# First attention of a two-layer encoder: values as the stationary operand, probabilities normalised before their transposition

## The chip, the cores and the metric

The kernel runs on one core of one Trainium2 chip. The metric is the device time of one execution in microseconds (us). Five engines of the core work side by side and meet at semaphores: TensorE (PE: matrix products, with its weight loads shown as PEld), VectorE (DVE), ScalarE (ACT), GpSimd (POOL) and SyncE (SP, which here starts the loads of weights).

## The reference

A two-layer encoder over 512 tokens with 1024 features, 16 heads of 64. Layer 0 has neighbourhood attention over a grid of 8 rows and 64 columns of tokens, layer 1 sliding-window attention with 4 key and value heads, and each is followed by a squared-ReLU MLP. The first attention is what the change touches:

```python
def neighbourhood_attention(h, w_qkv, rpb, w_o):
    ...
    def row_block(args):
        ...
        s = jnp.einsum('bchd,brckhd->bhcrk', q_r, k_win).astype(jnp.float32)
        ...
        s = s + bias[None].astype(jnp.float32)
        p = jax.nn.softmax(s.reshape(B, N_HEADS, GRID_W, kr * NA_COLS), axis=-1)
        p = p.reshape(B, N_HEADS, GRID_W, kr, NA_COLS).astype(v.dtype)
        return jnp.einsum('bhcrk,brckhd->bchd', p, v_win)
    ...
    return jnp.einsum('bsd,de->bse', o, w_o)
```

Each token sees a window of 8 by 16 grid tokens around it. Results are float32.

## The kernel before

**Numbers in two parts.** Every operand of a product is kept as a high part (`w_hi`, `pt_hi`, ...), which is a cast to the product's type, and a low part (`w_lo`, `pt_lo`, ...), the rest. A product is then high x high + low x high + high x low. ScalarE makes high parts, VectorE low parts, so each operand passes through both.

**Weights.** All weight matrices come as one stream of 180 chunks (128 x 1024) through two buffers `w_raw`. SyncE loads them, ScalarE casts (`w_hi`), VectorE subtracts (`w_lo`); both functions are called `split_weights`. TensorE uses a chunk in 24 products of 512 columns into one of two accumulators `acc`.

**The first attention** is done in steps. Step m makes the query, key and value rows of head pair m (three weight chunks, 3m to 3m+2, `dense_part(0)` to `dense_part(2)`), and does the attention of pair m-1 between these chunks. Steps 1 to 8 attend; step 8 has no chunks of its own but the first part of the output projection in their place. A pair is done in two units g = 0 and 1. A unit is two query tiles j of 128 queries for both heads hh, so four blocks of 128 queries by 256 keys.

For a unit TensorE makes the scores (`na_scores`, into `s_ps`), VectorE adds the bias and finds the largest (`na_logits`), ScalarE takes the exponentials and their sums `rsum` (`na_exp`, in `na_probs`), TensorE transposes the probabilities in eight blocks (`na_transpose`, into `pt_ps`), ScalarE and VectorE split them (`pt_high`, `pt_low`), and TensorE multiplies them with V (`na_values`). The value rows `vT` are transposed to token order in two batches (`na_v_blocks`, into the bank `misc_ps`), and split (`v_high`, `v_low`). In `na_values` the transposed probabilities are the stationary operand, in 16 products of 128 or 64 columns into the bank `o_ps`. VectorE then adds the two halves and divides by the sums (`na_o_sum`: a reciprocal, a reduction, a multiplication into `o_tok`), TensorE transposes the result back to feature order (`transpose_o`), and both engines split it into the operand of the output projection (`na_o_high`, `na_o_low`).

**Order.** Each engine works off one list of instructions, written out by hand in `na_step` of that engine; there is no scheduler. A wait stops everything behind it on its engine. A number such as `o_summed >= 2p` is counted by the semaphore that `then_inc` raises. After step 8, TensorE makes a small table product for the second attention (`t5_product`, in `misc_ps`), then goes on with the output projection.

## Time and profile before

| | us |
|---|---|
| three runs | 1174.11, 1174.2, 1174.97 (median 1174.2) |
| profiled execution | 1175.7 |
| its span, from first to last instruction | 1174.0 |
| TensorE busy in it | 1150.0 |
| VectorE busy | 623.4 |
| ScalarE busy | 466.4 |
| GpSimd busy | 129.6 |
| one step of the first attention (scores to scores, 110.99 to 136.25) | 25.26 |
| mean granted clock of TensorE | 0.996 of full |

The first attention takes the span from about 32 to 235 us. A product's row in a timeline lasts longer than the interval to the next one, since products are pipelined: what a block costs is read from start to start. Busy shares are means over the whole span and say nothing about a block; the waits and the timeline of a step do.

### The profile page before, as it was taken

How to read it: one execution, taken by the hardware profiler on the slowest of the kernel's cores; microseconds unless marked ns; L12 is line 12 of the kernel's file. 1: busy time of each engine (PE TensorE's matmuls, PEld its weight loads, DVE VectorE, ACT ScalarE, POOL GpSimd, SP SyncE). 2: the span in 40 equal slices, each digit the busy share in tenths (PEclk: the TensorE clock that was granted, in tenths of full speed). 3: DMA queues.
4: the chain of work that ended last, by engine and by line, in shares of the span. 5: the costliest groups of instructions: out<-in, count | busy, mean ns of one | idle time of the engine just before them, and what ended most of it. 6: DMA issues, size and time to landing. Idle time of an engine off the chain costs nothing.

```text
span 1174.0 us, 16835 instructions
## 1 busy us (share of the span) xinstructions
PE 1150.0 (98%) x5770; PEld 949.1 (81%) x5770; DVE 623.4 (53%) x988; ACT 466.4 (40%) x811; POOL 129.6 (11%) x243
## 2 busy tenths in 40 slices
PE   6999999999999999999999999999999999999996
PEld 4788888877888888888888788887888888888886
DVE  7676666575443324444345788766544233454335
ACT  6445545344342213433223666644443122443221
POOL 4734332050000000000000122100000000000000
PEclk9999999999999999999999999999999999999998
DMA  7422221142223223232232122122222323223222
GB/s 199 119 70 83 67 85 54 56 133 94 104 89 106 92 91 106 89 103 85 98 107 90 51 63 63 34 71 90 104 93 90 107 89 104 92 90 106 90 89 90
DMA packets 36850, 106.74 MB, mean 91 GB/s; under 512 B 8224, under 2 KB 10544, under 8 KB 36816
## 3 DMA queue, kind: packets, MB, share of 16 engines
q1 hardware_dynamic: 31680, 98.98, 25.2%
q0 software_dynamic: 4992, 7.29, 2.8%
q8 instruction: 21, 0.34, 0.1%
q14 instruction: 13, 0.11, 0.0%
q10 hardware_dynamic: 144, 0.02, 0.0%
HBM read 102.92 MB, written 3.34 MB: 91 GB/s over the span
## 4 chain that ended last, share of the span: by engine, by line
PE 91%; DVE 3%; issue 1%; POOL 1%; ACT 1%; SPq 1%; DMA 1%; DVEq 0%; ACTq 0%; POOLq 0%
PE acc L364 26%; PE acc L366 25%; PE acc L365 25%; PE s_ps L436 3%; PE o_ps L469 2%; PE o_ps L466 2%; PE pt_ps L626 1%; PE pt_ps L457 1%; DVE w_lo L967 1%; SPq L262 1%; PE misc_ps L469 1%; PE misc_ps L426 1%; POOL bias_pairs L292 1%; PE s_ps L364 1%; PE misc_ps L466 1%
## 5 line engine op out<-in xcount | busy, mean ns | idle before, releaser
L721 ACT CAST w_hi<-w_raw 128x1024 fp32r<-128x1024 f32 x180 | 188.8, 1049 | 416.4 <-PE acc L366 412.5
L364 PE MATMUL acc<-h_hi,w_hi 128*128 128x512 f32 x800 | 324.4, 406 | 10.3 <-DVE sqsum L984 9.8
L366 PE MATMUL acc<-h_hi,w_lo 128*128 128x512 f32 x800 | 313.4, 392 | 0.0
L365 PE MATMUL acc<-h_lo,w_hi 128*128 128x512 f32 x800 | 313.0, 391 | 0.0
L967 DVE TENSOR_TENSOR w_lo<-w_raw,w_hi 128x1024 fp32r<-128x1024 f32 x180 | 221.4, 1230 | 153.1 <-ACT w_hi L721 153.0
L364 PE MATMUL acc<-u_hi,w_hi 128*128 128x512 f32 (+1 forms) x624 | 241.4, 387 | 0.9 <-DVE w_lo L967 0.9
L366 PE MATMUL acc<-u_hi,w_lo 128*128 128x512 f32 (+1 forms) x624 | 239.5, 384 | 0.0
L365 PE MATMUL acc<-u_lo,w_hi 128*128 128x512 f32 (+1 forms) x624 | 239.4, 384 | 0.0
L364 PEld LDWEIGHTS acc<-h_hi,w_hi 128*128 128x128 f32 x800 | 150.9, 189 | 48.6 <-issue 14.2
L366 PEld LDWEIGHTS acc<-h_hi,w_lo 128*128 128x128 f32 x800 | 150.9, 189 | 32.4
L365 PEld LDWEIGHTS acc<-h_lo,w_hi 128*128 128x128 f32 x800 | 151.4, 189 | 29.0 <-issue 1.2
L995 DVE SCALAR_TENSOR_TENSOR scaled<-acc,rstd 128x512 f32<-128x512 f32 x90 | 62.2, 691 | 162.1 <-PE acc L366 161.4
L364 PEld LDWEIGHTS acc<-u_hi,w_hi 128*128 128x128 f32 x624 | 117.2, 188 | 26.0 <-DVE w_lo L967 2.6
L366 PEld LDWEIGHTS acc<-u_hi,w_lo 128*128 128x128 f32 x624 | 117.2, 188 | 23.2
L365 PEld LDWEIGHTS acc<-u_lo,w_hi 128*128 128x128 f32 x624 | 117.3, 188 | 22.5
L765 ACT ACTIVATE probs<-probs,nmax 128x256 f32<-128x256 f32 (+1 forms) x128 | 67.8, 531 | 62.5 <-DVE nmax L1055 62.5
L314 POOL DMA_DIRECT2D bias_pairs<-t_shifted x64 | 32.4, 508 | 466.2 <-ACT esink L895 458.5
L1107 DVE TENSOR_TENSOR x_res<-acc,x_res 128x512 f32 (+1 forms) x39 | 26.9, 691 | 101.1 <-PE acc L366 101.1
L1005 DVE TENSOR_TENSOR u_lo<-scaled,u_hi 128x512 f32 (+1 forms) x80 | 55.3, 691 | 12.6 <-ACT u_hi L757 12.2
L304 POOL TENSOR_TENSOR bias_masked<-bias_pairs,mask 128x256 f32<-128x256 f32 x64 | 45.3, 748 | 91.3 <-DVE nmax L1055 89.3
L757 ACT CAST u_hi<-scaled 128x512 f32 (+1 forms) x80 | 49.7, 621 | 10.2 <-DVE scaled L995 3.0
L1015 DVE TENSOR_TENSOR pt_lo<-pt_ps,pt_hi 128x1024 fp32r<-128x1024 f32 (+2 forms) x48 | 45.8, 954 | 13.1 <-ACT pt_hi L770 13.1
(105 smaller groups left out, 989.1 us busy)
## 6 DMA issues: line engine op xcount, KB each, us to landing
w_raw<-in_wstream SPq DMA_DIRECT2D x180, 512.0 KB, 3.3
bias_pairs<-rpb_shifted POOLq DMA_DIRECT2D x64, 48.0 KB, 3.0
bias_pairs<-t_shifted POOLq DMA_DIRECT2D x64, 48.0 KB, 2.1
x_res<-in_xT SPq DMA_DIRECT2D x8, 256.0 KB, 4.6
out_y<-x_res SPq DMA_DIRECT2D x16, 128.0 KB, 1.8
t_shifted<-vT POOLq DMA_DIRECT2D x16, 31.0 KB, 2.0
rpb_shifted<-rpb_pad SPq DMA_DIRECT2D x8, 45.0 KB, 8.5
rpb_shifted<-rpb_pad POOLq DMA_DIRECT2D x8, 45.0 KB, 5.3
```

Source lines behind the costliest of these rows:

```text
L304: ins = nc.gpsimd.tensor_tensor(bias_m[:, g, i, :, :].rearrange("p c r -> p r c"), rows[:, :, U0[j]:U0[j] + WC], mask[:, j:j + 1, :].to_br ...
L364: nc.tensor.matmul(dst, a[0], b[0], start=start, stop=False)
L365: nc.tensor.matmul(dst, a[0], b[1], start=False, stop=False)
L366: return nc.tensor.matmul(dst, a[1], b[0], start=False, stop=stop)
L436: ins = nc.tensor.matmul(dst(hh), a[s, queries[0], queries[1]], b[s, keys[0], keys[1]], start=start, stop=stop)
L721: nc.scalar.copy(w_hi[:, c.odd, :], w_raw[:, c.odd, :]).then_inc(w_hi_made, 1)
L757: nc.scalar.copy(dst, src).then_inc(tile_hi, 1)
L765: return nc.scalar.activation(src, src, ACT.Exp, bias=nmax[:, slot, i:i + 1], scale=-1.0, accum_out=rsum[:, slot, i:i + 1])
L967: nc.vector.tensor_tensor(w_lo[:, c.odd, :], w_raw[:, c.odd, :], f32(w_hi[:, c.odd, :]), ALU.subtract).then_inc(w_split, 1)
L995: nc.vector.scalar_tensor_tensor(out=dst, in0=order(acc[g.odd][:]), scalar=factor, in1=order(rstd[:]), op0=op, op1=ALU.mult).then_inc(acc_ ...
L1005: nc.vector.tensor_tensor(order[0](dst), order[1](scaled[:, e.odd, :]), order[0](f32(hi)), ALU.subtract).then_inc(tile_split, 1)
L1015: nc.vector.tensor_tensor(pt_lo[:, 0:blocks, :], pt_ps[:, 0:blocks, :], f32(pt_hi[:, 0:blocks, :]), ALU.subtract).then_inc(pt_split, 1)
```

## The change

- `na_values`: the values, high and low part of one head side by side, are the stationary operand (128 columns), and both parts of the transposed probabilities the moving one (2 x 128 columns). A unit takes 8 products of 256 columns. All four combinations of parts come out, in four corners of a block with features down the partitions; the corner low x low isn't used. A unit's outputs now lie in both banks, `o_ps` and `misc_ps`, which become one tile `om_ps`.
- Since outputs already have features on the partitions, `transpose_o` goes for this attention. The corners that lie on the other half of the partitions are copied across by ScalarE (`na_o_shift`, two copies of 64 x 256), and VectorE sums the three corners in four additions on half of the partitions each (`na_o_sum`).
- The division by the sums moves to before the transposition: VectorE's reciprocal (`na_inverse`), then four scaled copies in place by ScalarE (`na_normalise`).
- The exponentials of a unit wait for its first two logits, not all four.
- Because a values block writes both banks, the V transpositions and the table product wait until the outputs before them were read (`outputs_read`, on `o_summed`), and `na_values` of a first unit waits for both V batches.
- The order on the engines is rewritten to fit.

```diff
-        v_hi, v_lo = v_parts[:, :, :, 0, :], v_parts[:, :, :, 1, :]
+        v_quarters = v_parts[:].rearrange("p n h t d -> p n (h t) d")
+        v_hi, v_lo = v_quarters[:, :, 0:4:3, :], v_quarters[:, :, 1:3, :]
...
-        pt_hi, pt_lo = sb("pt_hi", [P, 8, P], F32R), sb("pt_lo", [P, 8, P], F32R)
+        pt_parts = sb("pt_parts", [P, 2, 8, P], F32R)
+        pt_hi, pt_lo = pt_parts[:, 0, :, :], pt_parts[:, 1, :, :]
...
-        o_ps = ctx.enter_context(nc.psum_tensor("o_ps", [P, QT, P], F32))
-        misc_ps = ctx.enter_context(nc.psum_tensor("misc_ps", [P, QT, P], F32))
+        om_ps = ctx.enter_context(nc.psum_tensor("om_ps", [P, 2, QT, P], F32))
+        o_ps, misc_ps = om_ps[:, 0, :, :], om_ps[:, 1, :, :]
...
+            def outputs_read(units):
+                pe.wait_ge(o_summed, units.v)
+
             def na_values(p, g):
                 unit = p * 2 + g
                 pe.wait_ge(pt_split, (unit + 1).v)
-                pe.wait_ge(v_split, (unit + 1).v)
+                pe.wait_ge(v_split, (p * 2 + 2).v)
                 if unit.a >= 1:
-                    pe.wait_ge(o_split, unit.v)
-                for i in range(4):
-                    hh, j = i // 2, 2 * g + i % 2
-                    ins = values(o_ps[:, i, :], [2 * i, 2 * i + 1], [2 * j, 2 * j + 1], hh)
+                    outputs_read(unit)
+                for jj in range(2):
+                    for hh in range(2):
+                        for b in range(2):
+                            ins = nc.tensor.matmul(om_ps[:, jj, 2 * hh:2 * hh + 2, :],
+                                                   v_parts[:, 2 * (2 * g + jj) + b, hh, :, :].rearrange("p a b -> p (a b)"),
+                                                   pt_parts[:, :, 2 * (2 * hh + jj) + b, :], start=b == 0, stop=b == 1)
                 ins.then_inc(pv_done, 1)
...
                     if p.a >= 1:
                         pe.wait_ge(v_split, (p * 2).v)
+                        outputs_read(p * 2)
...
                     na_scores(p, 0)
+                    dense_part(0, 0)
                     na_v_blocks(p, 0)
-                if attend and before:
-                    dense_part(0, 0)
-                    transpose_o(p * 2 + -1, o_ps)
                     dense_part(0, 1)
...
                     na_transpose(p, 1)
-                    dense_part(2, 0)
-                    transpose_o(p * 2, o_ps)
-                    dense_part(2, 1)
+                dense_part(2)
+                if attend:
                     na_values(p, 1)
...
             pe.wait_ge(table_landed, 16 * 2)
+            outputs_read(At(UNITS_NA))
...
+            def na_o_shift(p, g):
+
+                unit = p * 2 + g
+                act.wait_ge(pv_done, (unit + 1).v)
+                if unit.a >= 1:
+                    act.wait_ge(o_summed, unit.v)
+                nc.scalar.copy(o_far[TOP, :, :], om_ps[BOTTOM, :, 0, :])
+                nc.scalar.copy(o_far[BOTTOM, :, :], om_ps[TOP, :, 2, :]).then_inc(o_shifted, 1)
...
             def na_exp(p, g):
                 unit = p * 2 + g
-                act.wait_ge(logits_made, (unit + 1).v)
+                act.wait_ge(na_first_logits, (unit + 1).v)
                 for i in range(4):
+                    if i == 2:
+                        act.wait_ge(logits_made, (unit + 1).v)
                     ins = exponent(na_probs[:, i, :], g, i)
+                ins.then_inc(exp_made, 1)
+
+            def na_normalise(p, g):
+                unit = p * 2 + g
+                act.wait_ge(den_made, (unit + 1).v)
+                for i in range(4):
+                    ins = nc.scalar.activation(na_probs[:, i, :], na_probs[:, i, :], ACT.Copy,
+                                               scale=rden[:, g, i // 2, i % 2, :])
                 ins.then_inc(probs_made, 1)
...
+            def na_inverse(p, g):
+                unit = p * 2 + g
+                dve.wait_ge(exp_made, (unit + 1).v)
+                nc.vector.reciprocal(dens_of(rden, g), rsum[:, g, :]).then_inc(den_made, 1)
+
             def na_o_sum(p, g):
                 unit = p * 2 + g
-
-                def dens(g):
-                    nc.vector.reciprocal(dens_of(rden, g), rsum[:, g, :]).then_inc(den_made, 1)
-                    dve.wait_ge(den_made, (unit + 1).v)
-
-                o_sum(unit, unit, g, o_ps, dens)
+                dve.wait_ge(pv_done, (unit + 1).v)
+                dve.wait_ge(o_shifted, (unit + 1).v)
+                if unit.a >= 1:
+                    dve.wait_ge(o_split, unit.v)
+                nc.vector.tensor_tensor(o_t[TOP, :, :], om_ps[TOP, :, 0, :], o_far[TOP, :, :], ALU.add)
+                nc.vector.tensor_tensor(o_t[BOTTOM, :, :], om_ps[BOTTOM, :, 3, :], o_far[BOTTOM, :, :],
+                                        ALU.add).then_inc(o_added, 1)
+                dve.wait_ge(o_added, (unit + 1).v)
+                nc.vector.tensor_tensor(o_t[TOP, :, :], om_ps[TOP, :, 1, :], o_t[TOP, :, :], ALU.add)
+                nc.vector.tensor_tensor(o_t[BOTTOM, :, :], om_ps[BOTTOM, :, 2, :], o_t[BOTTOM, :, :],
+                                        ALU.add).then_inc(o_summed, 1)
...
             def na_step(m, dense=True, attend=True, before=True):
                 p, c, g = m + -1, m * 3 + CH_NA, m * 3 + GR_NA
                 if attend:
+                    na_logits(p, 0)
                     if before:
                         na_o_sum(p + -1, 1)
-                    na_logits(p, 0)
-                    v_low(p * 2, slice(0, 4))
+                    na_inverse(p, 0)
                     if before:
                         na_o_low(p + -1, 1)
+                    v_low(p * 2, slice(0, 4))
...
                     scale_tile(c, g, e, HD ** -0.5)
-                    split_weights(c + 2)
-                    tile_low(e, u_lo[:, 8 + m.odd, :], u_hi[:, 8 + m.odd, :], (in_tiles, by_tile))
                 if attend:
+                    na_logits(p, 1)
                     pt_low(p * 2, 8)
                     v_low(p * 2 + 1, slice(4, 8))
-                    na_logits(p, 1)
                 if dense:
+                    split_weights(c + 2)
+                if attend:
+                    na_inverse(p, 1)
+                if dense:
+                    tile_low(e, u_lo[:, 8 + m.odd, :], u_hi[:, 8 + m.odd, :], (in_tiles, by_tile))
```

Here is how the order moves at two places. First TensorE at the start of a step from the second on, from the pair's first scores to the second half of the first chunk. L436 (before) and L442 (after) are the scores, L426 and L432 the V transpositions, L478 the output transpositions; a chunk's products are three rows per block. Before:

```order
L436 MATMUL s_ps<-k_hi,u_lo 128x256 x2
L494 ISA
L426 MATMUL misc_ps<-ident,vT 128x128 x4
L377 REGISTER_ALU
L379 REGISTER_ALU
L364 MATMUL acc<-h_hi,w_hi 128x512
```

And the end of that half chunk, before:

```order
L366 MATMUL acc<-h_hi,w_lo 128x512
L478 MATMUL o_ps<-ident,o_tok 128x128 x2
L364 MATMUL acc<-h_hi,w_hi 128x512
```

After:

```order
L442 MATMUL s_ps<-k_hi,u_lo 128x256 x2
L383 ISA
L385 REGISTER_ALU
L370 MATMUL acc<-h_hi,w_hi 128x512
```

And the end of that half chunk, after:

```order
L372 MATMUL acc<-h_hi,w_lo 128x512
L507 REGISTER_ALU
L432 MATMUL om_ps<-ident,vT 128x128 x4
L370 MATMUL acc<-h_hi,w_hi 128x512
```

The V transpositions have moved from right behind the scores to the middle of the first chunk, where the output transpositions were; those are gone.

Second VectorE at the same place, from the weight split that ends the step before. L1055 and L1089 are logits (two rows each), L1023 and L1025 the old sum and division, L1073 to L1078 the new additions. Before (the step's first rows):

```order
L1045 RECIPROCAL rden<-rsum 128x4 [waits pv_done]
L1023 TENSOR_REDUCE o_raw<-o_ps 128x256 [waits den_made]
L1025 TENSOR_TENSOR o_tok<-o_raw,rden 128x2x2x64 [waits o_added]
L1060 REGISTER_ALU
L1055 ISA probs,nmax<-s_ps,bias_masked 128x256 [waits pt_done,scores_done,bias_made]
```

After (from the last of the four logits on):

```order
L1089 ISA probs,nmax<-s_ps,bias_masked 128x256
L1089 ISA nmax 128x1
L1072 REGISTER_ALU [waits o_shifted,pv_done]
L1073 TENSOR_TENSOR o_tok<-om_ps,o_raw 64x256 [waits o_split]
L1074 TENSOR_TENSOR o_tok<-om_ps,o_raw 64x256
L1077 TENSOR_TENSOR o_tok<-om_ps,o_tok 64x256 [waits o_added]
L1078 TENSOR_TENSOR o_tok<-om_ps,o_tok 64x256
L1065 RECIPROCAL rden<-rsum 128x4 [waits exp_made]
L1084 ISA [waits o_hi_made]
```

The previous unit's sum has moved from ahead of the new pair's logits to behind them, and is four instructions where it was two and a reciprocal.

## Rows read from the trace of the kernel before

**Rows 1.** The page's busy times: engine, busy us, share of span, instructions.

```profile
PE 1150.0 (98%) x5770; PEld 949.1 (81%) x5770; DVE 623.4 (53%) x988; ACT 466.4 (40%) x811; POOL 129.6 (11%) x243
```

**Rows 2.** Waits of TensorE, 20 to 220 us: total, times, longest.

```profile
PE pt_ps L457 <- ACT probs L765: 2.0, 1, 2.0
PE o_ps L478 <- DVE o_tok L1025: 0.5, 1, 0.5
PE misc_ps L426 <- DVE vT L995: 0.3, 1, 0.3
```

**Rows 3.** Timeline of TensorE, one step: start, duration, line, what, count.

```profile
94.30 0.39 PE L436 MATMUL s_ps<-k_hi,u_hi 64*128 64x256 f32 x2
...
95.21 0.50 PE L364 MATMUL acc<-h_hi,w_hi 128*128 128x512 f32 x1
95.55 0.40 PE L365 MATMUL acc<-h_lo,w_hi 128*128 128x512 f32 x1
...
100.78 0.22 PE L469 MATMUL o_ps<-v_parts,pt_hi 128*128 128x128 f32 x1
...
102.52 1.06 PE L457 MATMUL pt_ps<-ident,probs 128*128 128x128 f32 x8
103.33 0.48 PE L364 MATMUL acc<-h_hi,w_hi 128*128 128x512 f32 x1
...
105.94 0.39 PE L366 MATMUL acc<-h_hi,w_lo 128*128 128x512 f32 x1
...
106.62 0.40 PE L365 MATMUL acc<-h_lo,w_hi 128*128 128x512 f32 x1
...
109.16 0.22 PE L469 MATMUL o_ps<-v_parts,pt_hi 128*128 128x128 f32 x1
...
110.99 0.39 PE L436 MATMUL s_ps<-k_hi,u_hi 64*128 64x256 f32 x2
```

**Rows 4.** Timeline of VectorE, the same step and the next one's start.

```profile
103.34 1.25 DVE L1005 TENSOR_TENSOR k_lo<-scaled,k_hi 128x512 fp32r<-128x512 f32 x1
...
105.75 1.22 DVE L1015 TENSOR_TENSOR pt_lo<-pt_ps,pt_hi 128x1024 fp32r<-128x1024 f32 x1
...
110.44 1.23 DVE L967 TENSOR_TENSOR w_lo<-w_raw,w_hi 128x1024 fp32r<-128x1024 f32 x1
111.58 0.17 DVE L1045 RECIPROCAL rden<-rsum 128x4 f32<-128x4 f32 x1
...
112.87 0.42 DVE L1055 CUSTOM_DVE_ANT_0 probs<-s_ps,bias_masked 128x256 f32<-128x256 f32 x1
...
114.25 0.69 DVE L1010 TENSOR_TENSOR v_parts<-misc_ps,v_parts 128x512 fp32r<-128x512 f32 x1
```

**Rows 5.** Groups by line, 0 to 240 us: busy us, mean ns of one.

```profile
L1023 DVE TENSOR_REDUCE o_raw<-o_ps 128x256 f32<-128x512 f32 x16 | 11.1, 692 | 0.6
...
L1036 DVE TENSOR_TENSOR u_lo<-o_ps,u_hi 128x256 f32 (+1 forms) x16 | 6.8, 424 | 16.0 <-ACT u_hi L780 15.9
L780 ACT CAST u_hi<-o_ps 128x256 f32 (+1 forms) x16 | 5.8, 364 | 22.5 <-PE o_ps L478 22.5
```

**Rows 6.** Timeline of ScalarE, an exponential and the reading of its accumulator.

```profile
89.17 0.51 ACT L765 ACTIVATE probs<-probs,nmax 128x256 f32<-128x256 f32 x1 [1.25 <-DVE nmax L1055]
89.59 0.18 ACT L765 ACTIVATION_READ_ACCUMULATOR probs<-probs,nmax 128x1 f32 x1
```

**Rows 7.** Timeline of VectorE and TensorE in the first attending step.

```profile
38.01 0.42 DVE L1055 CUSTOM_DVE_ANT_0 probs<-s_ps,bias_masked 128x256 f32<-128x256 f32 x1 [2.89 <-POOL bias_masked L304]
...
50.90 2.33 DVE L967 TENSOR_TENSOR w_lo<-w_raw,w_hi 128x1024 fp32r<-128x1024 f32 x1 [0.32 <-ACT w_hi L721]
...
41.64 1.09 PE L457 MATMUL pt_ps<-ident,probs 128*128 128x128 f32 x8 [2.03 <-ACT probs L765]
```

**Rows 8.** Timeline of TensorE, the table product behind the last values block.

```profile
234.56 0.60 PE L686 MATMUL misc_ps<-onehot_sb,table 32*16 32x257 f32 x2
```

**Rows 9.** Busy times around the first step's stop; after POOL: PEclk, DMA share, GB/s.

```profile
39.60:45.00 5.40, 3.37 (x29) 2.91 (x29) 3.52 (x5) 4.83 (x12) 3.80 (x8) 1.00 0.24 46
```

More of the change, by code:

```diff
@@ L214, in encoder @@
         last_square = probs[:, SEQ:2 * SEQ]
+        o_far = o_raw[:].rearrange("p h j d -> p (h j d)").rearrange("p (j n) -> p j n", j=2)
+        o_t = o_tok[:].rearrange("p h j d -> p (h j d)").rearrange("p (j n) -> p j n", j=2)
+        TOP, BOTTOM = slice(0, HD), slice(HD, P)
         na_probs = probs[:, 0:QT * ROWS * WC].rearrange("p (j n) -> p j n", j=QT)
@@ L465, in low @@
                     def low():
-                        nc.tensor.matmul(dst[:, 0:HD], pt_lo[:, t, :], v_hi[:, n, hh, :], start=False, stop=False)
+                        nc.tensor.matmul(dst[:, HD * hh:HD * (hh + 1)], pt_lo[:, t, :], v_hi[:, n, hh, :], start=False,
+                                         stop=False)
                     if b:
@@ L532, in na_step @@
                     na_transpose(p, 1)
-                    dense_part(2, 0)
-                    transpose_o(p * 2, o_ps)
-                    dense_part(2, 1)
+                dense_part(2)
+                if attend:
                     na_values(p, 1)
-                else:
-                    dense_part(2)
             def output_projection(ch, gr, heads_before, start, bank):
                 early_part(ch, gr, heads_before, start, LAST_OUT)
-                transpose_o(At(heads_before + HEADS - 1), bank)
+                if bank is not None:
+                    transpose_o(At(heads_before + HEADS - 1), bank)
                 early_part(ch, gr, heads_before, LAST_OUT, len(EARLY_BLOCKS))
@@ L794, in na_step @@
                 if attend:
-                    v_high(p * 2, v_hi[:, 0:4, :, :])
+                    if before:
+                        na_o_shift(p + -1, 1)
                     na_exp(p, 0)
@@ L798, in na_step @@
                         na_o_high(p + -1, 1)
+                    na_normalise(p, 0)
+                    v_high(p * 2, v_hi[:, 0:4, :, :])
+                if dense and m.a == 0:
+                    load_sqrt()
+                    deviation(0)
+                if attend:
+                    pt_high(p * 2, 8)
+                    v_high(p * 2 + 1, v_hi[:, 4:8, :, :])
                 if dense:
-                    if m.a == 0:
-                        load_sqrt()
-                        deviation(0)
                     split_weights(c + 2)
@@ L901, in sw_o_high @@
             def sw_o_high(p, g):
-                o_high(p * 2 + (HEADS + g), p, g, False, sw_bank(g))
+                act.wait_ge(ot_done, (p * 2 + (g + 1)).v)
+                nc.scalar.copy(half_blocks(u_hi[:, p.v, :], g), flat(sw_bank(g)[:, 0:2, :])).then_inc(o_hi_made, 1)
             def sw_step(m, before=True, dense=True):
@@ L935, in _ @@
             na_step(At(8), dense=False)
+            na_o_shift(At(7), 1)
             na_o_high(At(7), 1)
@@ L1026, in o_sum @@
                                         rden[:, g, :, :, :].to_broadcast([P, 2, 2, HD]), ALU.mult).then_inc(o_summed, 1)
-            def o_low(done, tile, g, grid, bank):
-                dve.wait_ge(o_hi_made, (done + 1).v)
-                hi, lo, src = f32(u_hi[:, tile.v, :]), u_lo[:, tile.v, :], bank[:, 0:2, :]
-                if grid:
-                    hi, lo = half_tiles(hi, g), half_tiles(lo, g)
-                    src = src.rearrange("p j (r c) -> p j r c", c=QC)
-                else:
-                    hi, lo, src = half_blocks(hi, g), half_blocks(lo, g), flat(src)
-                nc.vector.tensor_tensor(lo, src, hi, ALU.subtract).then_inc(o_split, 1)
```

34 lines of the change are left out of this document (19 added, 15 removed).

## The prediction

> **What bounds the kernel now.** I read the page's busy times first: TensorE is busy 1150.0 of 1174.0 us [rows 1]. That alone doesn't say that it is never late, so I read its waits in the first 200 us after the start, where the first attention lies: three, 2.0, 0.5 and 0.3 us, all of them in the first head pair [rows 2]. From the second pair on TensorE goes from block to block without a gap: one step (one head pair and three weight chunks) takes the 25.26 us of the table above. So a TensorE microsecond that goes is worth a microsecond, until another engine's work comes late. Both have to be counted, since the change shortens TensorE's part and lengthens what VectorE and ScalarE do between its blocks.
>
> **What the change takes from TensorE.** The values block has 16 products, each with a stationary operand of its own, and takes 1.74 us from its first product to the transpositions behind it [rows 3]: 0.109 each. It becomes 8 products of 256 columns. No row shows such a product on 128 rows. From below it costs the 0.109 at which products with fresh stationary operands follow each other now, from above the 0.2275 of a 512-column product (5.57 us for 24, the first interval 0.11 longer, 0.34 [rows 3]). I take half of the latter, 0.114, as the columns are half: 0.91 for the block, **0.83 less**, twice a step. The two transpositions of an output stand between two products whose starts are 0.68 us apart [rows 3] where two plain intervals give 0.46: **0.22 less**, twice a step.
>
> **What waits in its place, at the start of a step.** The four V transpositions move behind half a chunk, and they now need the previous unit's outputs read, because the new values block writes their bank too. Count from the first product of a pair's second values block (109.16 [rows 3]). TensorE would be there after 0.91 (values), 0.09 (the passage to the scores: 110.99 - 109.16 less 1.74), 0.91 (scores [rows 3]) and 2.84 (12 products at 0.228 and a 0.11 longer first interval): 4.75. VectorE: it scales the V rows, splits a weight chunk, and is free at 2.42 (111.58 [rows 4]). The logits of the new pair now come first, four in 1.38 us (112.87 to 114.25 [rows 4]): 3.80, as their scores are done before that. Behind them stand the four half-width additions, which the trace doesn't have. The nearest is the 256-element subtraction that reads PSUM, 0.424 [rows 5], in which 128 partitions or 64 should not matter. From below each costs the 0.345 at which the logits follow each other [rows 4], from above the 0.69 of a reduction over 512 [rows 5]. I take 0.424 for all four, as if none overlapped: 1.70 and 0.04 for the wait in their middle, 5.54, and TensorE starts at 5.59. ScalarE's two shifting copies are no part of this: they start when the values are done (1.1), cost some 0.36 each as today's 256-element copy of an output does [rows 5] and are over at 1.85.
>
> That is a new stop of 0.84 us. From the start of the second values block to the middle of the next chunk, the V transpositions left out on both sides, the old order needs 1.83 + 0.91 + 2.74 and 0.22 for the output transpositions = 5.70, the new one 5.59. So the first half of a step gives **only 0.11**, its stop eats the rest. It occurs seven times (steps 2 to 8).
>
> On the overlap of VectorE's additions the Trainium skill has a rule (VectorE: DVE Perf Modes, section "Two Vector instructions with no wait between them"): an instruction whose operand or output begins in another 32-partition quadrant than the last one's in that memory starts only when all earlier ones have finished. The additions alternate between partitions 0 and 64, so by the rule 0.424 stands; by the 0.345 interval of the rows the chain would be up to 0.3 shorter. No run here shows the rule yet.
>
> **The other two chains.** Second unit of a step, counted from the trace's step at 94.30: TensorE reaches its transpositions 0.91 + 5.57 + 0.91 = 7.39 after the scores begin. Scores are done at 1.1, logits at 2.5 (VectorE takes them before the splits now), the exponentials begin when ScalarE has done the casts ahead of them, near 2.6, and end near 4.6. The reciprocal is queued behind the logits, the P subtraction (1.13), the V one (0.60) and a weight split (1.14 [rows 4]): 5.4, done 5.6. The four normalisations are a scaled copy, which the trace doesn't have either; an exponential is followed by the reading of its accumulator after 0.42 [rows 6]. I take 0.40 each and 0.09 for the last one's end, from above the whole 0.51 of an exponential [rows 6]: done at 7.3. **Slack 0.1**. Then the K side: ScalarE's weight cast follows the normalisations (1.05), VectorE splits (1.14), subtracts K (at most 1.25 [rows 4]), adds (1.74), subtracts P (1.22 [rows 4]): about 6.4 after 7.3, and TensorE wants that P after 0.81 of transpositions (102.52 to 103.33) and 5.61 of products (5.83 to 109.16 less 0.22 [rows 3]), at 7.39 + 6.42 = 13.8. **Slack 0.1 to 0.3.** So the second half of a step gives its full 0.83 + 0.22 = **1.05**, eight times, but with almost nothing in hand. The first unit's normalised values are ready 1.3 before they are wanted, since the stop comes before them. GpSimd's masked bias still starts on the logits' end, and SyncE's weight loads on the splits, of which only the third chunk's comes later, by 4 us, two chunks ahead of its use.
>
> **First step, last step, end.** In the first step the logits come late, at 38.01, and TensorE already waits for the exponentials, till 41.64 [rows 7]. Now they may begin after two logits (38.8) and end at 40.9; reciprocal and normalisations bring 42.8: +1.2. The V split follows on both engines: +0.4. A weight split took 2.33 there [rows 7], which the 0.2 of slack doesn't hold: +0.4. The waits of 0.34 and 0.49 [rows 2] go. Without the weight chunks of a full step the last one has less in hand: +0.3. At the end the table product, which went straight behind the last values block, without a wait [rows 8], waits for the outputs: values done 1.1, shifts 1.85, additions 3.6, against an arrival at 1.0: +2.6, less the 0.83 and 0.22 of this last block: +1.55. During such a stop the clock could fall; the 2.0 us stop of the first step left it at 1.00 [rows 9].
>
> **Sum:** 7 x -0.11 = -0.8; 8 x -1.05 = -8.4; first step -0.83 + 2.0 = +1.2; last step +0.3; end +1.55: **-6.2 us**. The later stages keep their work. Against the profiled execution (1175.7 in all, span 1174.0) that is 1169.5; the median of the runs shown, 1174.2, is 1.5 lower, so 1168.0.
>
> **The rivals.**
> - *Additions overlap* (0.345 each): the first chain is 0.32 shorter, seven times and once at the end, -2.5: 1165.5. For it: every run of VectorE instructions in the rows overlaps. Against: a wait in their middle and changing partitions.
> - *The stops don't show at all*, because the chains are shorter than I count: -0.84 x 7, -2.6, -1.6 and -0.3 more: about 1157.5. Against: the first chain is nearly all rows, 3.80 of its 5.59.
> - *Normalisation binds*: 0.49 each instead of 0.40 makes the second unit 0.26 late past its slack and the K side with it, 8 x 0.3 = +2.4, and a tenth of a microsecond in extra sequencer work per chain does another 1.5: 1170.5 to 1172.5. Against: 0.42 in the row. For: the slack of 0.1.
> - *The other side, slower: half-width additions cost more than full-width ones.* Four stand in the first chain and four on the K side, and each extra x costs 4x at once in the first, 4x - 0.2 in the second: 7 x 4x + 8 x (4x - 0.2) + 4x. It is 6.2 at x = 0.12, so from 0.55 per addition on the change loses; at the 0.69 bound it costs 16: near 1182. For it: nothing in the rows but that the form is new.
> - *A 256-column product costs what a 512-column one does*, its moving operand being two runs of 128: 0.118 x 8 = 0.94 per block, eight times exposed and a little in the other ones: +9, 1177. It decides from 0.19 on. Against: scores products of 256 columns go in pairs, 12 in 0.91 us [rows 3].
>
> **How the numbers follow.** Forecast (stops as counted, additions between 0.36 and 0.45): 0.60, own range 1165.5 to 1170.5. Additions overlapping fully 0.11; no stops 0.06; normalisation binding 0.14, of it a third above 1171.9; slower additions 0.05; dear products 0.04. This measurement can tell about 0.2%, 2.35 us, from no change. Faster, below 1171.9, is then 0.60 + 0.11 + 0.06 + 0.09 = 0.86, of which I take 0.04 off for late work that I haven't seen: 0.82. The two slower cases begin within 0.2%: slower 0.08, the rest, 0.10, within it. The range goes from 1162.0, halfway into the case without stops, to 1172.5, the end of the normalisation case.
>
> **What the changed profile would show.** Values blocks 0.9 us from first product to what follows; no TensorE row that reads o_tok; TensorE waiting 0.7 to 1.0 us for VectorE's o_tok before the first V transpositions, seven times, and 2.6 once before the table product; a period of 24.1 us; waits for probs or P near 0 after the first step, 1.2 in it. Additions at 0.42, starting 0.42 apart; normalisations starting 0.40 apart. The forecast is wrong if the additions or normalisations show other intervals, if a 256-column product is not near 0.114, or if a weight split comes late (I see none: the one now behind the logits ends some 3 us before its chunk).

## The result, and the profile after

The changed kernel takes 1177.84 us (median of 20 runs, 1174.47 to 1179.34), the kernel before 1175.26 (20 runs, 1174.1 to 1176.55): ratio 1.0022, interval 1.0016 to 1.0028. It is slower by 0.22%, where 1168.0 was forecast. (The forecast stood on the three runs of before that are shown above, median 1174.2; the 20 runs have 1175.26, so 1.06 of the miss is the base.) One of the twelve runs of the experiment `e_inverse` took 2926.36 us; its ratio to before leaves that run out, its median of 1173.72 doesn't (the other eleven have 1173.36). TensorE has less to do, as the page's busy row says beside [rows 1], and yet the span grew from 1174.0 to 1176.5:

```profile
PE 1140.4 (97%) x5610; PEld 935.5 (80%) x5610; DVE 639.7 (54%) x1020; ACT 505.2 (43%) x907; POOL 134.7 (11%) x243
```

So 9.6 us of TensorE's busy time went and 12 us of waiting came. Its waits in the changed kernel between 20 and 240 us (total, times, longest), beside [rows 2]:

```profile
PE pt_ps L463 <- ACT probs L811: 5.9, 8, 3.8
PE om_ps L432 <- DVE o_tok L1078: 5.3, 7, 0.8
PE om_ps L697 <- DVE o_tok L1078: 2.8, 1, 2.8
```

The second and third line are the stops that the prediction counted. Of the first line 3.8 stand in the first step, forecast as 3.2 (its 2.03 and 1.2 more); the other seven waits, 0.2 to 0.6 each, were forecast as none. One step on TensorE's timeline, beside [rows 3]:

```profile
97.17 0.39 PE L442 MATMUL s_ps<-k_hi,u_hi 64*128 64x256 f32 x2
...
103.65 1.11 PE L500 MATMUL om_ps<-pt_parts,v_parts 128*128 128x256 f32 x8
105.04 1.09 PE L463 MATMUL pt_ps<-ident,probs 128*128 128x128 f32 x8 [0.28 <-ACT probs L811]
...
111.44 1.11 PE L500 MATMUL om_ps<-pt_parts,v_parts 128*128 128x256 f32 x8
112.48 0.39 PE L442 MATMUL s_ps<-k_hi,u_hi 64*128 64x256 f32 x2
...
116.02 0.39 PE L372 MATMUL acc<-h_hi,w_lo 128*128 128x512 f32 x1
117.13 0.63 PE L432 MATMUL om_ps<-ident,vT 128*128 128x128 f32 x4 [0.72 <-DVE o_tok L1078]
```

From the second values block to the scores it is 1.04 (111.44 to 112.48), where it was 1.83, and to the V transpositions 5.69 (forecast 5.59). But the second unit's transpositions start 1.39 after the values block (103.65 to 105.04) instead of 0.91: 0.48 late, though the row shows only 0.28 of it as idle, since the end of a product's row lies behind the start of the next one. Why it is late, VectorE's and GpSimd's timelines show, beside [rows 4]; the last row gives the four biases' shortest, median and longest time in ns, and when the first and the last of them begin:

```profile
101.50 1.66 DVE L998 TENSOR_TENSOR w_lo<-w_raw,w_hi 128x1024 fp32r<-128x1024 f32 x1
103.08 0.17 DVE L1065 RECIPROCAL rden<-rsum 128x4 f32<-128x4 f32 x1
103.17 1.14 DVE L1036 TENSOR_TENSOR u_lo<-scaled,u_hi 128x512 fp32r<-128x512 f32 x1
...
109.09 0.42 DVE L1077 TENSOR_TENSOR o_tok<-om_ps,o_tok 64x256 f32<-64x256 f32 x1
109.52 0.43 DVE L1078 TENSOR_TENSOR o_tok<-om_ps,o_tok 64x256 f32<-64x256 f32 x1
```
```profile
99.93 3.84 POOL L310 TENSOR_TENSOR bias_masked<-bias_pairs,mask 128x256 f32<-128x256 f32 x4 [6.28 <-DVE nmax L1089]
```
```profile
L310 POOL TENSOR_TENSOR bias_masked<-bias_pairs,mask x4: 751/754/1743, 99.9 to 102.0; 128x256 f32<-128x256 f32 x4
```

GpSimd's masked biases (bias plus mask, four additions of 0.75 each) run from 99.93. VectorE's weight split, 1.23 elsewhere, begins at 101.50, during the third of them, and takes 1.66; the third ends near 102.07, and the split 1.09 later. So it stands still until the third bias has ended. The fourth, begun at 102.0, stands still until the split has ended (1743 ns), and the U subtraction behind the split takes 1.14, not 0.68, in the same way. The reciprocal, which the change makes the way to the second unit's probabilities, is queued behind the split. In the kernel before, the biases ran from 99.19 to 102.03, and the next split began at 102.20. The Trainium skill (SBUF — State Buffer, section "Who interferes with whom") says that a VectorE instruction with two SBUF inputs contends with a GpSimd one that reads SBUF, and that one blocks while the other has the port. By that rule, this trace agrees: each of the two waits out the other here.

The clock fell twice. Windows (busy time with counts of TensorE, its weight loads, VectorE, ScalarE, GpSimd; then TensorE's granted clock, DMA share, GB/s), beside the 1.00 of [rows 9]:

```profile
39.00:45.00 6.00, 2.25 (x11) 1.75 (x10) 2.31 (x11) 4.25 (x13) 4.49 (x9) 0.78 0.11 25
45.00:50.00 5.00, 5.00 (x25) 4.11 (x24) 2.11 (x10) 3.90 (x8) 4.66 (x9) 0.58 0.23 54
50.00:55.00 5.00, 5.00 (x27) 4.25 (x25) 5.00 (x6) 2.13 (x9) 4.12 (x8) 1.00 0.06 10
230.00:235.00 5.00, 2.89 (x16) 2.14 (x14) 4.25 (x7) 2.10 (x4) 0.00 (x0) 1.00 0.40 137
235.00:240.00 5.00, 4.35 (x13) 3.17 (x14) 2.30 (x6) 0.40 (x1) 2.95 (x7) 0.70 0.27 89
```

The first fall is in and behind a stop of 3.75 us, the second behind the one ahead of the table product. TensorE's timeline there, beside [rows 8]: products are 0.43 apart from 236.97 to 240.38, the 1.2 GHz level, where they were 0.23 apart:

```profile
235.65 0.59 PE L697 MATMUL om_ps<-onehot_sb,table 32*16 32x257 f32 x2 [2.77 <-DVE o_tok L1078]
...
237.39 0.63 PE L371 MATMUL s_ps<-u_lo,w_hi 128*128 128x512 f32 x1
237.82 0.63 PE L372 MATMUL s_ps<-u_hi,w_lo 128*128 128x512 f32 x1
```

The first attending step, beside [rows 7], on GpSimd, VectorE and TensorE:

```profile
47.22 5.62 POOL L310 TENSOR_TENSOR bias_masked<-bias_pairs,mask 128x256 f32<-128x256 f32 x8
```
```profile
51.37 2.54 DVE L998 TENSOR_TENSOR w_lo<-w_raw,w_hi 128x1024 fp32r<-128x1024 f32 x1
53.83 0.16 DVE L1065 RECIPROCAL rden<-rsum 128x4 f32<-128x4 f32 x1
```
```profile
43.62 1.97 PE L463 MATMUL pt_ps<-ident,probs 128*128 128x128 f32 x8 [3.75 <-ACT probs L811]
55.79 1.10 PE L463 MATMUL pt_ps<-ident,probs 128*128 128x128 f32 x8 [0.55 <-ACT probs L811]
```

**Where the time went.** The span can be cut at four starts that every trace has: VectorE's first logits, the second step's first scores, the eighth step's first scores (six periods later), and ScalarE's `rstd` of the next norm. What lies behind the last is 902.0 to 902.1 in every kernel.

| | before | after | difference | forecast |
|---|---|---|---|---|
| start to first logits | 38.01 | 38.73 | +0.72 | 0 |
| first logits to second step | 22.48 | 24.52 | +2.04 | -0.7 |
| six periods | 6 x 25.26 | 6 x 24.63 | -3.79 | -7.0 |
| eighth step to `rstd` | 59.96 | 63.47 | +3.51 | +1.5 |

The forecast column is the prediction's sum by these bounds: first step +1.2 - 1.05 - 0.83; periods 6 x -1.16; the rest +0.72 - 1.05 + 0.3 + 1.55. The first row can't be told from the chance of one execution: the first logits wait for GpSimd's biases and those for a DMA, and in the traces of kernels with the same instructions up to there they begin between 36.5 and 38.9.

### The profile page after: what moved, and what is told of

It reads as the page before. It is cut to its first block, busy times and chain, and to the rows that moved or that the text cites. A ratio compares the mean times of both kernels' runs of the same rounds, so it can differ in the third digit from the quotient of the medians.

```text
span 1176.5 us, 16678 instructions
## 1 busy us (share of the span) xinstructions
PE 1140.4 (97%) x5610; PEld 935.5 (80%) x5610; DVE 639.7 (54%) x1020; ACT 505.2 (43%) x907; POOL 134.7 (11%) x243
## 4 chain that ended last, share of the span: by engine, by line
PE 85%; DVE 7%; issue 3%; ACT 2%; POOL 1%; SPq 1%; DMA 1%; DVEq 0%; ACTq 0%; POOLq 0%
PE acc L370 24%; PE acc L371 24%; PE acc L372 24%; PE s_ps L442 3%; DVE probs L1089 2%; PE om_ps L476 2%; PE pt_ps L636 1%; PE pt_ps L463 1%; PE om_ps L472 1%; DVE w_lo L998 1%; ACT probs L811 1%; SPq L268 1%; DVE pt_parts L1046 1%; PE om_ps L432 1%; PE s_ps L370 1%
## 5 line engine op out<-in xcount | busy, mean ns | idle before, releaser
L370 PE MATMUL acc<-h_hi,w_hi 128*128 128x512 f32 x800 | 324.1, 405 | 10.9 <-DVE sqsum L1015 10.4
L998 DVE TENSOR_TENSOR w_lo<-w_raw,w_hi 128x1024 fp32r<-128x1024 f32 x180 | 224.2, 1245 | 155.7 <-ACT w_hi L732 155.6
L1036 DVE TENSOR_TENSOR u_lo<-scaled,u_hi 128x512 f32 (+1 forms) x80 | 58.0, 725 | 12.6 <-ACT u_hi L768 12.2
L310 POOL TENSOR_TENSOR bias_masked<-bias_pairs,mask 128x256 f32<-128x256 f32 x64 | 51.2, 839 | 85.2 <-DVE nmax L1089 82.0
L742 ACT ACTIVATE h_hi<-x_res,gain 128x512 fp32r<-128x512 f32 (+1 forms) x32 | 23.1, 722 | 71.3 <-DVE x_res L1147 62.9
```

The costliest lines, as they stand in the source:

```text
L310: ins = nc.gpsimd.tensor_tensor(bias_m[:, g, i, :, :].rearrange("p c r -> p r c"), rows[:, :, U0[j]:U0[j] + WC], mask[:, j:j + 1, :].to_br ...
L370: nc.tensor.matmul(dst, a[0], b[0], start=start, stop=False)
L998: nc.vector.tensor_tensor(w_lo[:, c.odd, :], w_raw[:, c.odd, :], f32(w_hi[:, c.odd, :]), ALU.subtract).then_inc(w_split, 1)
L1036: nc.vector.tensor_tensor(order[0](dst), order[1](scaled[:, e.odd, :]), order[0](f32(hi)), ALU.subtract).then_inc(tile_split, 1)
```

## The experiments

Unless it says otherwise each is the changed kernel with the edit shown. Medians stand against 1177.84, and the medians of the kernel before that were measured beside them lie between 1175.09 and 1175.43; "first step" and "end" are the second and fourth row of the table above (24.52 and 63.47 for the changed kernel).

| run | median, us | ratio to before (95%) | first step | period | end |
|---|---|---|---|---|---|
| e_fill | 1176.45 | 1.0016 (1.0007 to 1.0024) | 24.54 | 24.63 | 61.74 |
| e_table | 1173.77 | 0.9987 (0.9979 to 0.9996) | 24.55 | 24.62 | 59.13 |
| e_step1 | 1179.62 | 1.0037 (1.0024 to 1.005) | 26.36 | 24.63 | 64.88 |
| e_inverse | 1173.72 | 0.9984 (0.9974 to 0.9993) | 23.50 | 24.14 | 63.43 |
| e_bias | 1175.27 | 0.9998 (0.9989 to 1.0007) | 23.66 | 24.51 | 64.73 |
| e_si | 1172.91 | 0.9981 (0.9972 to 0.999) | 23.00 | 24.14 | 63.42 |
| e_vlate | 1166.94 | 0.9935 (0.9921 to 0.9948) | 24.55 | 23.22 | 62.04 |
| e_best | 1160.56 | 0.9875 (0.986 to 0.989) | 23.50 | 23.12 | 57.73 |
| e_fill_end | 1175.73 | 1.0005 (0.9996 to 1.0014) | 24.52 | 24.63 | 61.75 |
| e_fill_inv | 1172.59 | 0.9974 (0.9964 to 0.9985) | 23.02 | 24.14 | 64.71 |
| e_best2 | 1159.87 | 0.9874 (0.9858 to 0.9889) | 21.01 | 23.13 | 57.72 |
| b_step1 (of before) | 1175.87 | 1.0 (0.9991 to 1.0009) | 22.45 | 25.25 | 59.97 |

**e_fill: work in both long stops.**

```
+            def fill(count):
+                for _ in range(count):
+                    nc.tensor.matmul(flat(pt_ps[:, 0:4, :]), h_hi[:, 0, 0:P], h_hi[:, 0, :], start=True, stop=True)
...
+                    if not before:
+                        fill(15)
                     na_transpose(p, 0)
...
             pe.wait_ge(table_landed, 16 * 2)
+            fill(11)
             outputs_read(At(UNITS_NA))
```

> The changed kernel, with products added whose result nothing reads: 15 of 512 columns while TensorE waits 3.75 us for the first step's probabilities, 11 while it waits 2.77 us ahead of the table product. No wait is removed. Theory 1 (the clock): these two stops left the granted clock at 0.78 and 0.58 in the first step and at 0.70 after the table product; kept busy, TensorE stays near 1.00, the 8 transpositions of the first step take about 1.0 instead of 1.97, and 2.4 + 1.6 = 4.0 us come back: about 1173.8. Rival (the stops cost their own length only, and the work after them is slow for another reason): no change, 1177 to 1178, with the same slow products at about 0.43 behind both.

Measured: -1.4, a third of it. Windows of the trace:

```profile
45.00:50.00 5.00, 5.00 (x24) 4.12 (x23) 5.00 (x11) 2.72 (x10) 4.98 (x8) 1.00 0.10 23
...
235.00:240.00 5.00, 5.00 (x24) 4.12 (x23) 1.93 (x3) 1.05 (x1) 4.97 (x11) 1.00 0.24 52
```

The clock stayed at 1.00 in both places (0.58 and 0.70 without the filling). The end is 1.7 shorter, but the first step is as long as it was (24.54). What TensorE gained there it lost at the second transposition, since the split, started earlier, now stands still for longer (VectorE, then TensorE):

```profile
46.02 1.22 DVE L1053 TENSOR_TENSOR pt_parts<-pt_ps,pt_parts 128x1024 fp32r<-128x1024 f32 x1
...
47.76 4.22 DVE L1005 TENSOR_TENSOR w_lo<-w_raw,w_hi 128x1024 fp32r<-128x1024 f32 x1
```
```profile
53.86 1.09 PE L463 MATMUL pt_ps<-ident,probs 128*128 128x128 f32 x8 [2.83 <-ACT probs L818]
```

Theory 1 falls for the first step and stands for the end. In the twelve traces with GpSimd's eight biases in a row (two of them of the old order), that split ends 1.06 to 1.09 after the last of them, whenever it began: 52.84 and 53.91 in the changed kernel, 50.89 and 51.98 here. As it takes 1.21 to 1.23 alone, it gets next to nothing done while they run. Not every VectorE instruction is held up so: the P subtraction at 46.02, beside the same eight biases (45.28 to 50.89), took its usual 1.22. One of its inputs lies in PSUM, where both inputs of the split lie in SBUF.

**e_fill_end: the end's stop alone filled** (the `fill(11)` of above).

> The changed kernel with 11 products of 512 columns, whose result nothing reads, in the 2.8 us stop ahead of the table product, and nothing else: the stop stays as long, but TensorE has work in it. Theory 1 (the clock): the products behind it run 0.23 apart and not 0.43, and -1.6 us comes back: about 1176.2. Rival (the fall is not what costs): 1177.8. The table product later gave -4.1; with the stop at 2.8, the clock's share would then be the rest, 1.3.

Measured: -2.1, and 1.7 in the profile's end. The clock's price behind this stop is 1.7 of 3.51.

**e_table: the table product behind five blocks of the output projection.**

```
             def output_projection(ch, gr, heads_before, start, bank):
                 early_part(ch, gr, heads_before, start, LAST_OUT)
+                if bank is None:
+                    pe.wait_ge(table_landed, 16 * 2)
+                    outputs_read(At(UNITS_NA))
+                    nc.tensor.matmul(flat(misc_ps[:])[0:HEADS, 0:RELS], table[:], onehot_sb[:], start=True,
+                                     stop=True).then_inc(t5_product, 1)
```

> The changed kernel with one edit: the table product moved behind five blocks of the output projection, so that TensorE has work while the last outputs are added up. Theory 1: the 2.77 us stop goes and the clock's fall of 1.6 us with it: -4.2 us, about 1173.6. If the stop costs its length only: -2.7 us, 1175.1. Rival (the end is bound by something else, such as the table's rows that are written and read back): no change.

Measured: -4.1, in the profile -4.34 at the end, as the theory has it: 1.7 of clock and 2.6 of stop. The end is then 0.8 shorter than before the change.

**e_step1: half of a dense part ahead of the first step's first transposition.**

```
+                if attend and not before:
+                    dense_part(1, 0)
                 if attend:
                     na_transpose(p, 0)
...
-                dense_part(1)
+                if attend and not before:
+                    dense_part(1, 1)
+                else:
+                    dense_part(1)
```

> The changed kernel with one edit, in the first attention step alone: four of the eight pieces of the second dense part come ahead of the first transposition, not behind it. Theory 1: the 3.75 us stop shrinks by their 2.5 to 3 us to about 1 and the clock stays near 1.00: -2.4 for the clock, and up to -2.7 of the stop where nothing later waits in its place: -4 to -5 us, about 1173. Rival (the stop is set by a chain that ends the step anyway, and the clock doesn't matter): -1 or less, with a new wait later in the step.

Measured: +1.8, a miss. The first transposition waits 0.84 only, but the second one, with its cover moved ahead, waits behind a split of 4.19, and now the clock falls behind that stop, where nothing hides it:

```profile
54.18 1.97 PE L463 MATMUL pt_ps<-ident,probs 128*128 128x128 f32 x8 [4.66 <-ACT probs L816]
```
```profile
50.00:55.00 5.00, 0.82 (x4) 0.82 (x5) 3.56 (x4) 2.58 (x6) 3.82 (x8) 0.62 0.36 104
```

Its rival was right: a chain through the other engines ends this step. The second transposition starts 17.09 after the first logits here, 17.11 in e_fill and 17.06 in the changed kernel, whatever TensorE did before it. The 1.8 more come behind it: products at half the clock, with the stop ahead of them 4.66 long, where e_fill had 2.83 and full clock.

**e_inverse: the second unit's reciprocal ahead of the split.**

```
-                if dense:
-                    split_weights(c + 2)
                 if attend:
                     na_inverse(p, 1)
                 if dense:
+                    split_weights(c + 2)
                     tile_low(e, u_lo[:, 8 + m.odd, :], u_hi[:, 8 + m.odd, :], (in_tiles, by_tile))
```

> The changed kernel with one edit: on VectorE the second unit's reciprocal comes ahead of the weight split that took 1.66 us and held it. Theory 2 (the second unit's probabilities are late because this short reciprocal stands behind the stretched split): the start of the second transposition moves forward by about 0.45 us in each of 7 or 8 steps, the short waits ahead of it go, -3.0 to -3.6 us, about 1174.5. Rival A (the exponentials on ScalarE end too late anyway): no change. Rival B (the weight split, now later, holds up the next split or the products that read it): slower, with a new wait on w_lo.

Measured: -4.1. The period falls by 0.483, the lateness read above, and between 60 and 230 us TensorE's waits are one line; that for `probs` is gone:

```profile
PE om_ps L432 <- DVE o_tok L1078: 5.2, 7, 0.8
```

The first step, too, is 1.0 shorter. Rival A falls: the exponentials were in time. The split itself did not move: it ends 3.23 after the first bias begins, in this kernel (97.25 to 100.48) as in the changed one (99.93 to 103.16); only what was queued behind it is free.

**e_bias: GpSimd's second masked bias one unit of logits later.**

```
-                    pool.wait_ge(logits_made, (pair * 2 + (g - 1)).v)
+                    pool.wait_ge(logits_made, (pair * 2 + (1 if g else -1)).v)
```

> The changed kernel with one edit: GpSimd's masked bias of the second unit waits for one unit of logits more, so that it no longer runs beside VectorE's weight split. Theory 2 in full (the split took 1.66 instead of 1.23 us, and 4.2 in the first step of two other kernels, because GpSimd works on SBUF at the same time and one stands still while the other runs): the split is back at 1.23, the reciprocal behind it comes 0.43 earlier, the waits of 0.25 ahead of the second transposition go, and some 0.4 us in each of 7 steps come back: -3 us, about 1175. Rival (the stretch has another cause, such as the reads of TensorE or a DMA): the split still takes 1.66 and the time stays at 1177.8. If the masked biases now meet another VectorE operation that binds: slower.

Measured: -2.6, but the period gave only 0.12 of the 0.4. The biases were held up by the loads ahead of them in GpSimd's queue, and met the same split from the other side: they end at 100.38, and the split again 1.07 later (GpSimd, VectorE). In the first step, where GpSimd does nothing at that time, the split took 1.21:

```profile
97.54 2.84 POOL L310 TENSOR_TENSOR bias_masked<-bias_pairs,mask 128x256 f32<-128x256 f32 x4
```
```profile
50.60 1.21 DVE L998 TENSOR_TENSOR w_lo<-w_raw,w_hi 128x1024 fp32r<-128x1024 f32 x1
...
99.81 1.64 DVE L998 TENSOR_TENSOR w_lo<-w_raw,w_hi 128x1024 fp32r<-128x1024 f32 x1
```

The cause of the stretch is shown by this pair and by the unmoved 1.07; as a remedy for the later steps the edit failed.

**e_si: the edits of e_step1 and e_inverse together.**

> The changed kernel with two edits of earlier runs together: half of the first step's second dense part ahead of the first transposition, and the second unit's reciprocal ahead of the weight split. The first edit alone made it slower (1179.6), with a new stop of 4.66 us at the second transposition, whose reciprocal stood behind a split of 4.19 us that ran beside GpSimd's masked biases. If that is the cause, the reciprocal ahead of the split removes that stop, both long stops of the first step go, the clock stays at 1.00, and it is 4 to 5 us below the reciprocal edit alone (1173.7): about 1169. Rival (the first step is set by what GpSimd makes, whatever the order): within 1 us of 1173.7.

Measured: 0.8 below e_inverse alone, as the rival had it, not the forecast's 4 to 5. The 4.66 us stop is gone (0.56 is left), so it was the reciprocal behind the split. But the products that need the split then wait for it, 1.18 at `w_lo`, and the first step is 23.00, against 23.50.

**e_fill_inv: e_inverse with 16 filling products in the first step's stop.**

> The kernel with the reciprocal ahead of the split (1173.7), with 16 such products in the 4.2 us stop ahead of the first step's first transposition. The reciprocal no longer waits for the stretched split, so the stop at the second transposition that took back what the filling of both stops gave should be small. Theory 1: the clock stays at 1.00 in the first step, where it was 0.57 and 0.75, and -2.4 us comes back: about 1171.3. Rival (the first step ends with GpSimd's masked biases and the split behind them, whatever TensorE's clock): 1173 to 1174, with a wait for w_lo of about 1 us in place of it, as the kernel with both edits of the first step had it.

Measured: 1.1 below e_inverse; first step 23.02 against 23.50, with the clock at 1.00 there and 0.57 and 0.75 without. Once the reciprocal is free, the clock costs 0.5 in the first step, not 2.4.

**e_vlate: V transpositions behind the whole dense part.**

```
                     dense_part(0, 0)
-                    na_v_blocks(p, 0)
                     dense_part(0, 1)
+                    na_v_blocks(p, 0)
...
                     na_transpose(p, 0)
-                    na_v_blocks(p, 1)
                     na_scores(p, 1)
+                    na_v_blocks(p, 1)
```

> The changed kernel with one edit: in each step the first V transpositions come behind the whole first dense part, not in its middle, and the second ones behind the second unit's scores. The seven stops of 0.7 to 0.8 us at the step's start, in which TensorE waits for the output additions of 0.43 us apart, should go. If their cost is their length (as the prediction had it): -0.75 x 7 = -5.3 us, about 1172.5. Rival (a later wait takes their place, for the normalised probabilities or for the split V): half of it or less, with that wait in the list.

Measured: -10.9, twice the forecast. The period fell by 1.40: more than the 0.72 to 0.8 of the stop and the 0.11 longer first interval behind it. The rest, about 0.5, is the size of what e_inverse gave: the second unit's scores now come ahead of four V transpositions, and between them and the transposition that waited there is 0.5 us more of work. That this is the reason is argued and not shown by an edit of its own; the wait for `probs` is gone from the list, though the split still took 1.65 to 1.67 in the six later steps. Between 60 and 230 us one wait is left, ahead of the table product:

```profile
PE om_ps L697 <- DVE o_tok L1078: 2.8, 1, 2.8
```

**e_best: e_table, e_step1, e_inverse and e_vlate together.**

> The changed kernel with all four edits: table product later, half a dense part earlier in the first step, reciprocal ahead of the split, V transpositions later. If the four costs are separate they add up: -4.1 (table, measured) -4.1 (reciprocal, measured) -4.5 (first step, once the reciprocal is free) -5.3 (step starts) = -18: about 1160, and no wait over 1 us between 40 and 240 us. If they share one limit: 1165 or more.

Measured: 1160.56, the forecast's 1160. The trace has no wait of TensorE between 60 and 230 us; the period is 23.12, 0.11 less than with e_vlate alone, so most of what e_inverse gives a period (0.48) is in e_vlate's gain already. The sum of four came out right by luck: the first step gave 1.0 in the profile where 4.5 had been put down for it, and the later V transpositions gave about twice their 5.3. The first step still has stops of 1.45 and 1.90.

**e_best2: e_best and e_bias.**

> The kernel with all four edits (1160.6), and GpSimd's masked bias of the second unit one unit of logits later as well. In the first step this leaves GpSimd idle when the split runs, which took 1.21 us so instead of 3.5 to 4.2: the wait for w_lo (0.64) goes, and the four kernels' second unit is no longer held: -0.6 to -1.5 us, about 1159.5. Rival (the logits now wait for the bias, which comes later): slower, with VectorE idle until GpSimd's bias_masked.

Measured: 1159.87 (1159.02 to 1162.67), with e_best at 1160.56 (1160.19 to 1161.33): no difference that these runs tell. In the profile the first step is 21.01 instead of 23.50, the wait for `w_lo` is gone and its split took 1.20. But the profiled execution is the fastest of the four, with a mean clock of 0.998 where the others have 0.995 to 0.996, and part of the 2.5 is the clock, which fell in the profile of e_best alone.

**b_step1: the kernel before with the edit of e_step1.**

> The kernel BEFORE the change with the first step's edit alone: half of the second dense part ahead of the first transposition, where it had a stop of 2.03 us. It is the fair yardstick for what order alone gives without the change. If the stop costs its length: -2.0, about 1173.1. If the first step ends with GpSimd's masked biases and the split behind them: -0.5 or less. In either case the kernel of before keeps its period of 25.26 us a step, so that the 15 us of the four edits are not to be had without the change.

Measured: no change, first step 22.45 against 22.48. Its stop of 2.03 went, and one of 1.8 came later in the step, for the first unit's outputs:

```profile
PE o_ps L478 <- DVE o_tok L1030: 1.8, 1, 1.8
```

So that step's stop cost nothing before the change either.

## Why the prediction was wrong

**Right:** the products and the additions. The values block costs what was forecast; the additions start 0.42 to 0.47 apart and nothing of them overlaps, which rules out the two rivals on them, as the 1.04 does that of the dear product. By the rule of the Trainium skill that the prediction cites (VectorE: DVE Perf Modes, section "Two Vector instructions with no wait between them"), the trace agrees. Four normalisations take 1.71 us, as forecast, so the rival in which normalisation binds by its own length falls. The chain to the stop at a step's start is as forecast, 5.69 for 5.59 (a stop of 0.72 to 0.8 for 0.84), and e_vlate showed its cost in full. The eighth step up to its last values block takes 20.70 before (212.03 to 232.73) and 20.67 after (211.00 to 231.67), 0.03 less, where +0.72 - 1.05 + 0.3 gives the same; that step has no weight split in the way of its second reciprocal. One slip in the sums changes nothing: additions at the 0.69 bound cost 64 x 0.266 - 1.6 = 15.4, so that rival ends near 1183, not 1182.

**Wrong, step by step:**
1. "a weight split (1.14 [rows 4]): 5.4, done 5.6 ... **Slack 0.1**". The 1.14 was read where GpSimd is idle. The logits of the second unit now come ahead of the split, and it is they that release GpSimd's biases; so they run beside it. The split took 1.66, the reciprocal was late by 0.4, and 0.48 a period was lost: 6 x 0.48 = 2.9 of the 3.2 missed there. Putting the reciprocal first gave back 0.483. The prediction wrote that the bias "still starts on the logits' end" and didn't ask what VectorE would do then.
2. "A weight split took 2.33 there [rows 7] ... +0.4" in the first step. The 2.33 had the same cause; it ended 1.1 after GpSimd's biases. Before the change no probabilities were queued behind it. The step's end was set by the biases, split, reciprocal and normalisations in this order: 2.04 more instead of 0.7 less. The sum had put the late split at +0.4 in all. Neither the 3.75 stop nor the clock's fall behind it costs anything in the changed kernel (e_fill 24.54), and without the reciprocal in that queue the step is 1.0 to 1.5 shorter (e_inverse, e_fill_inv), with the biases away too, 3.5 in one profile (e_best2, with the other edits and in a fast execution; the medians of e_best and e_best2 don't tell the two apart).
3. "During such a stop the clock could fall; the 2.0 us stop of the first step left it at 1.00": the conclusion drawn for a stop of 2.6. It was 2.77 and the clock fell; 1.7 (e_fill_end) of the 2.0 missed at the end.

So step 1 and 2 have one cause, a queue behind an instruction that another engine holds up. They cost some 5.6 of the 8.0 by which the three lower rows of the table miss the forecast; the clock costs 1.7. My own first reading of the result, in which the clock cost 2.4 in the first step too, is refuted by e_fill. What stays open: why in the first step GpSimd's eight biases ran through ahead of the split, while in the later steps the split came in between the third and the fourth; and why, in some of the profiles, the fall at the end costs over 1 us more (end 64.7 to 64.9 in e_step1, e_bias and e_fill_inv).

The change itself was worth making: TensorE's work of a step fell from 25.26 to 23.12, which only shows when nothing waits. The kernel before has no gap in its periods to win by order [rows 2], and its first step didn't gain by it (b_step1). The four edits around the change make it 1.25% faster than before (ratio 0.9875, interval 0.986 to 0.989).

## What to carry to other kernels

When a short instruction becomes the way to the critical engine, look at what stands ahead of it in its queue, and put it ahead of any long one; its slack can't be summed from durations that were read where the engine beside it was idle. When an order moves, ask what its end releases, and which instruction will then run at the same time: in these traces VectorE's subtractions with two SBUF inputs and GpSimd's additions held each other up. A stop's length is its cost only if the next wait isn't already due: fill it and look whether the step gets shorter, before moving work for its sake.

## What the runs showed of the hardware

A VectorE split of 1.23 us (both inputs in SBUF) took up to 4.22 beside GpSimd's additions, and ended 1.06 to 1.09 after a run of them that it didn't get into; a subtraction with one input in PSUM took its usual 1.22 beside them. The granted clock fell behind stops of 2.77, 3.75 and 4.66 us, and not behind those of 0.8 or 2.03. But it stood at 1.00 behind the 2.83 of e_fill. Behind a stop of 1.90 it stood at 1.00 in e_best2 and fell in e_best, where another wait, of 0.64, follows within 2 us; products are 0.43 apart there from 53.87 to 56.86 (e_best, then e_best2):

```profile
51.20 1.09 PE L463 MATMUL pt_ps<-ident,probs 128*128 128x128 f32 x8 [1.90 <-ACT probs L817]
...
52.92 0.50 PE L370 MATMUL acc<-h_hi,w_hi 128*128 128x512 f32 x1 [0.64 <-DVE w_lo L1004]
```
```profile
50.00:55.00 5.00, 3.17 (x14) 2.57 (x15) 5.00 (x4) 2.97 (x5) 3.92 (x8) 0.85 0.24 64
```
```profile
50.00:55.00 5.00, 3.63 (x20) 3.17 (x21) 4.59 (x7) 4.94 (x9) 0.00 (x0) 1.00 0.41 122
```

So a stop's length alone doesn't say whether the clock falls: 2.77 and 2.83 came out differently, and what else decides isn't shown here.
